# A hybrid attention block on one core: in the second attention, TensorE's transposes of a step go ahead of the scores of the next step

## The reference, cut to what matters

```
def block(i):                      # 64 queries at a time, 8 heads of 64
    ...
    _, sel = lax.top_k(score, k_sel)          # 256 keys of each query
    valid = (sel // CHUNK) <= (qpos[None, :, None] // CHUNK)
    kg = gather(k, sel)
    vg = gather(v, sel)
    s = jnp.einsum('bqhd,bqkhd->bhqk', qb, kg).astype(jnp.float32) * scale
    ...
    s = jnp.where(valid[:, None], s + bias, -jnp.inf)
    p = jax.nn.softmax(s, axis=-1)
    return jnp.einsum('bhqk,bqkhd->bqhd', p.astype(v.dtype), vg)
```

## Time and profile before

| | before |
|---|---|
| median of 3 runs | 786.03 us (784.34 to 787.84) |
| profiled execution, its own time | 783.66 us |
| span of the profiled execution | 781.9 us |
| busy over the span: PE, PEld | 747.3 us, 629.6 us |
| busy over the span: DVE, ACT, POOL | 612.4 us, 305.2 us, 349.2 us |
| mean granted TensorE clock | 0.998 of full speed |

### The profile page before, as it was taken

How to read it: one execution, slowest core, us unless ns; L and a number is a source line. 1 busy time by engine, 2 the same in 40 slices (tenths; PEclk the granted TensorE clock), 3 DMA queues, 4 the chain that set the end, 5 groups by cost and what they waited for, 6 DMA issues and landing times.

```text
span 781.9 us, 11689 instructions
## 1 busy us (share of the span) xinstructions
PE 747.3 (96%) x4105; PEld 629.6 (81%) x4105; DVE 612.4 (78%) x1300; ACT 305.2 (39%) x677; POOL 349.2 (45%) x429
## 2 busy tenths in 40 slices
PE   3999999999999999999999999998999999899996
PEld 3765888888887888889888888887888898888885
DVE  4638999999999979978899999995767667524343
ACT  5437222130315666657521312106546455422221
POOL 5320121223538857751365553558999971300000
PEclk9999999999999999999999999999999999999999
DMA  7242111112220011040112112200202020212231
GB/s 277 61 122 67 41 42 54 48 47 54 68 54 0 1 41 28 14 115 10 42 46 63 42 53 55 68 14 27 69 15 82 2 82 1 84 65 85 77 109 54
DMA packets 24562, 44.56 MB, mean 57 GB/s; under 512 B 3076, under 2 KB 9912, under 8 KB 24376
## 3 DMA queue, kind: packets, MB, share of 16 engines
q1 hardware_dynamic: 24504, 43.81, 19.2%
HBM read 35.40 MB, written 6.57 MB: 54 GB/s over the span
## 4 chain that ended last, share of the span: by engine, by line
PE 60%; DVE 24%; POOL 8%; issue 3%; ACT 3%; DMA 1%; SPq 0%; DVEq 0%; POOLq 0%; ACTq 0%
PE psum L1131 22%; PE psum L1291 11%; DVE score L1456 9%; DVE top L1451 9%; PE psum L1230 8%; PE psum L1212 4%; PE psum L1190 3%; PE psum L1031 3%; PE psum L1059 3%; PE psum L1193 2%; PE psum L1075 2%; POOL k_high_twice L569 1%; POOL near_low L705 1%; ACT probsT_B L900 1%; POOL q_low_high L572 1%
## 5 line engine op out<-in xcount | busy, mean ns | idle before, releaser
L565 POOL TENSOR_TENSOR w_lo<-w_raw,w_hi 128x512 fp32r<-128x512 f32 x60 | 77.8, 1299 | 219.9 <-ACT w_hi L743 219.3
L1456 DVE MATCH_REPLACE8 score<-top,score 128x768 f32<-128x768 f32 (+5 forms) x176 | 157.3, 906 | 0.0
L1451 DVE MAX8 top<-score 128x8 f32<-128x768 f32 (+5 forms) x176 | 148.2, 909 | 1.0
L743 ACT ACTIVATE w_hi<-w_raw 128x512 fp32r<-128x512 f32 x60 | 37.7, 630 | 215.0 <-PE psum L1131 209.2
L889 ACT ACTIVATE probs<-psum,small 128x384 f32<-128x384 f32 (+7 forms) x128 | 94.8, 741 | 48.7 <-DVE small L1475 32.2
L1131 PE MATMUL psum<-w_hi,big_hi 128*128 128x512 f32 x256 | 99.6, 389 | 0.0
L1131 PE MATMUL psum<-w_hi,big_lo 128*128 128x512 f32 x256 | 99.6, 389 | 0.0
L1131 PE MATMUL psum<-w_lo,big_hi 128*128 128x512 f32 x256 | 99.6, 389 | 0.0
L1230 PE MATMUL psum<-v,probsT_B 128*128 128x64 f32 x576 | 75.8, 274 | 4.3 <-ACT probsT_B L900 3.5
L1230 PEld LDWEIGHTS psum<-v,probsT_B 128*128 128x128 f32 x576 | 70.5, 191 | 11.3 <-issue 4.0
L1131 PE MATMUL psum<-big_hi,w_hi 128*128 128x512 f32 x192 | 74.9, 390 | 0.0
(11 more groups left out here) (171 smaller groups left out, 1571.7 us busy)
## 6 DMA issues: line engine op xcount, KB each, us to landing
w_raw<-in_w_in SPq DMA_DIRECT2D x62, 256.0 KB, 2.6
xs<-in_x SPq DMA_DIRECT2D x8, 512.0 KB, 6.2
k_high_twice<-k_high_twice SPq DMA_DIRECT2D x16, 256.0 KB, 3.7
xres<-in_x SPq DMA_DIRECT2D x8, 512.0 KB, 3.7
out_y<-y_out SPq DMA_DIRECT2D x16, 256.0 KB, 2.1
w_tail<-in_w_out SPq DMA_DIRECT2D x10, 256.0 KB, 2.7
bias_scratch<-bias_row SPq DMA_DIRECT2D x1, 2304.0 KB
bias<-bias_scratch SPq DMA_DIRECT2D x12, 128.0 KB, 3.0
```

The source lines that it names most:

```text
L565: pool.tensor_tensor(lo[:, 0:cols], w_staged(n)[:, 0:cols], hi[:, 0:cols].bitcast(f32), ALU.subtract).then_inc(w_lo_made, 1)
L743: act.activation(w_parts(n)[0][:, 0:cols], w_staged(n)[:, 0:cols], ACT.Copy).then_inc(w_hi_made, 1)
L1451: ins = dve.max(top8[:, i - SEL0, :], sc)
L1456: ins = dve.match_replace(sc, top8[:, i - SEL0, :], sc, TAKEN)
```

## The change

`attend` is called for both attentions. For the second one (`ph == 1`), the scores of the first softmax of the next step no longer stand ahead of the transposes q0 and q1 of this step. They stand behind them, and with that directly ahead of the scores of the second softmax. The first attention keeps its order. No instruction is added or removed, and the queues of the other engines stay as they are.

```diff
                 for s in range(STEPS + lag):
                     t = s - lag
                     qs = quads[ph, t] if t >= 0 else []
-                    if s + 1 < STEPS:
+                    if ph == 0 and s + 1 < STEPS:
                         scores(ph, s + 1, 0)
                     if t == 0:
                         pe.wait_ge(bank_moved, moved[(A_GROUPS, B_GROUPS)[ph][-1] + 1])
                     for quad in qs[0:2]:
                         turn(ph, t, quad)
+                    if ph == 1 and s + 1 < STEPS:
+                        scores(ph, s + 1, 0)
                     if ph == 0 and s >= 1:
                         fill((s - 1) // DB, (s - 1) % DB)
                     if s + 1 < STEPS:
```

## The result

The changed kernel takes 796.08 us (794.83 to 796.77, 4 runs) against 786.93 us (784.34 to 788.58, 4 runs) in the runs beside it. The ratio is 1.0114, with a 95% interval from 1.0088 to 1.0139. That is 9.0 us slower, between 6.9 and 10.9. The forecast was 12.0 us slower, 798.0 us, with a range from 791.5 to 802.

The account below looks back on a forecast made before the run. TensorE was taken to bound the second attention, with VectorE paced by it. Four blocks losing 2.8 us each plus 0.8 in the first gave 12.0 us on 786.03, so 798.0 us, range 791.5 to 802.

Parts of the forecast that it names:

- i = 2: Block step with six transposes: VectorE's copy of q1 comes 1.16 us later, so the step ends late by 0.92 us.
- i = 4 and 6: Block steps where products wait for ScalarE's copy of q2 behind later exponentials: late by 2.22 and 2.82 us.
- i = 3: Block step with eight transposes: products wait for VectorE's later copy of q1, so it ends late by 0.64 us.
- i = 5: Block step where ScalarE's copy of q0 stands behind later m = 1 exponentials: no gain, late by 0.79 us.
- i = 0: Block step with two transposes, taken up by slack; the copy of q1 is late by 0.92, the step by 1.0 us.
- i = 1: Block step whose q1 transposes newly wait for the m = 1 exponentials: late by 1.86 us.
- i = 7: Block's 16-product step: copies late but still in time, lateness 2.8 us, which is the loss of a block.
- The first block: First block of the second attention: VectorE loses its lead, costing 0.8 us beyond the 2.8 us of each block.
- the clock as a rival: Short waits in the second attention lower TensorE's clock; one block at 1.2 GHz gives some 833 us; chance 2 in 100.
- the waits simply going: Second attention's 4.3 us of waits ahead of products vanish and none comes: 781.7 us; chance 4 in 100.
- the losses staying local: Only i = 3 and i = 1 pay, lateness is not handed on: 0.9 us a block, 789.8 us; chance 8 in 100.
- the full payment: Each step pays its transposes in full, no slack: 4.87 us a block, 805.5 us; chance 8 in 100.

Follow-up runs that it names:

- e11: The changed kernel plus 20 identity transposes filling TensorE's idle time before the second attention's first probabilities' transposes: median 795.0 us, 1.0115 of the kernel before.
- e12: The kernel before (old order) plus 14 identity transposes in TensorE's idle time at the second attention's start: median 785.12 us, 0.9991 of the kernel before.
- e5: The changed kernel with VectorE's far minimum cut to the first 128 keys, results not the reference's: 786.78 us, a block 35.62 us.
- e10: The kernel before with the new order only in step i = 3 of each block: 790.64 us in one run, a block 36.18 us.
- e4: The changed kernel with VectorE's copy of q1 put ahead of the far minimum and soften: 792.48 us in one run, a block 37.01 us.
- e2: The kernel before with the new order only in steps i = 4 and 6 of each block: 787.97 us in one run, a block 36.16 us.
- e8: The changed kernel with ScalarE's copy of q2 put ahead of the next m = 0 exponentials: 793.59 us in one run, a block 37.15 us.
- e1: The changed kernel with the old order kept in the first step of the second attention: 795.94 us, first block 39.20 us.
- e3: The kernel before with the new order only in steps i = 2 and i = 0 of each block: 786.68 us in one run, a block 35.24 us.

## Why the prediction was right, and where it was off

The sign, the place and the chain were right. The size was too large, mostly by one step (i = 2) and by the costs in i = 4 and 6: 12.0 us against 9.0 by the ratio of the runs (up to 10.9 by its interval), and against 9.8 for the stage at full clock (e11 against e12).

- **What bounds the kernel.** Right. VectorE, 69% busy in a block (24.61 of 35.44 us), needed its start more than its time. With a shorter chain on VectorE (e5) a block loses 0.42 us and not 2.27.
- **i = 3, late by 0.64.** Measured 0.60, and alone 0.58 (e10). The wait for the copy of q1 was the mechanism: e4 takes it away and with it 0.45 of the 0.60.
- **i = 5, late by 0.79 in all, so 0.15 more.** Measured 0.13.
- **i = 2, late by 0.92, so 0.13 more.** This step failed: it gained 0.19, a difference of 0.32 us a block. The prediction moved the copy of q1 by as much as `soften`. But before, the copy did not follow `soften` at once, as VectorE's order of time of the kernel before shows:

```profile
618.49 0.14 DVE L1501 DVE_READ_ACCUMULATOR2_ANT small<- 128x1 f32 x1
618.73 0.56 DVE L1518 COPY probsT_B<-psum 128x384 f32<-128x384 f32 x1
```

  `soften` had ended at 618.63, and the copy started at 618.73, right behind the end of the transposes (617.85 + 0.84 = 618.69). In the new order these are early, and the copy starts at 626.25, 1.25 us after the step's start, where it had been 1.14 (618.73 against 617.59). So the copy was 0.11 us later within its step, not 0.37, and TensorE no longer waited in the step (busy 2.58 of 2.58 us, where it had been 2.60 of 2.77). The row had been read for its end and not for what ended the gap ahead of it.
- **i = 0, 0.08 more; i = 1, 0.86 more.** Measured 0.18 and 0.74, together 0.92 against 0.94. The split differs because the first wait of i = 1 lies in i = 0's length.
- **i = 4, 0.36 more; i = 6, 0.60 more.** Measured 0.30 and 0.45, mis-sized by 0.21 together. In i = 6 of the changed kernel the copy of q2 starts at 643.79, 0.10 us before the exponential's accumulator read ends (643.70 + 0.19), and the step ends 1.66 us after the copy (644.38 to 646.04), not 1.7. e2 and e8 confirm the mechanism.
- **i = 7, taken as 0.02 less.** Measured 0.06 more.
- **The first block, 0.8 us more than the others.** Right: 3.03 for 2.27 at full clock. In the profiled run the clock took 1.35 us more (39.31 against e11's 37.96). The prediction had the clock as a rival for whole blocks and put it at 2 in 100 on the strength of a stretch that was 86% busy. What it missed is one idle time of 2.4 us, at a single place. Of its own signs of being wrong one thus came, a granted clock below 1.00 in this stage, but in the first step only. Of the waits for VectorE's copies that it named, those in i = 3 and 1 came (0.44 and 0.45 us), in i = 0 only the weight loads waited (0.26), and in i = 2 none did.

As for the rivals, neither the waits simply going nor the losses staying local nor the full payment came. The Trainium skill, "TensorE: Matmul & The Clock Gate", section "A second HAM failure mode: psum-queue depth-cycling", tells of a kernel whose clock went up and down because TensorE idled briefly and often. This stage has many short waits too. Behind the first step its clock stayed at 1.00, with TensorE 94% busy in a block (35.30 of 37.71 us), so here the trace does not show the like; its one fall stands behind a longer idle time.

## What to carry to other kernels

Before an instruction is moved on the engine that is the bound, ask which engine starts at its result and what stands behind that start in the other queue: here 0.8 us of transposes put ahead of some scores moved a whole chain of minimum, copy and exponential, and the bound engine came to wait at its end. An early producer is worth nothing where its consumer's engine is busy with something else at that time. And where steps differ in size, decide the order step by step: of eight steps one gained from this change, and two from a variant of it.

## What the runs showed of the hardware

At the start of the second attention of the changed kernel TensorE idled for 1.20 us, worked for 1.18, and idled for 2.43 us. Then it was granted 0.59 of its clock over 6.51 us, so for most of it the lower of the two levels, 1.2 GHz. A matmul of 512 columns was followed by the next after 0.43 us (540.80 to 541.23) instead of 0.23. The same place in the old order, with 1.7 us idle in place of 2.43, gave a clock of 1.00 in five profiles and 0.63 and 0.64 in two (e1, e3). So the same instructions at this place differ here from run to run, by 2.83 us over two steps between e3 and the kernel before. The runs of the kernel before beside e11 and e12 fit that: the four with a mean clock of 0.994 took 786.94 to 788.07 us, the other nine 784.36 to 785.84. Transposes of the identity put into the idle time went with a clock of 1.00 in both profiles of it.
